# A gated spatial mixing stage as one unrolled pipeline over eight PSUM banks, with post norms begun in the tails of the stages

## What is computed

```python
h = h + rmsnorm(y, post_g)              # post norm 0, after the mLSTM mixer
hn = rmsnorm(h, pre_g)                  # "pre1"
p = einsum('bsd,de->bse', hn, w_in)     # 1024 -> 3 x 2048
u, v, z = split(p)
u = gelu(u)
v = rmsnorm(gelu(v), sg_norm_g)         # over all 2048 columns
vg = v.reshape(B, 4, 128, 8, 256)       # 4 chunks of tokens, 8 groups of columns
wm = w_spatial * causal                 # 8 x 128 x 128
vs = einsum('gts,bcsgd->bctgd', wm, vg) + b_spatial
y = u * vs * silu(z)
y = einsum('bse,ed->bsd', y, w_out)     # 2048 -> 1024
h = h + rmsnorm(y, post_g)              # post norm 1, then out
```

## Time and profile before

| | us |
|---|---|
| median of 3 runs | 3165.85 (3164.73 to 3171.25) |
| the profiled execution | 3168.81 |
| its span | 3166.9 |
| TensorE busy in the span | 2781.3 (88%) |
| VectorE, ScalarE, GpSimd busy | 1460.2, 1097.8, 756.3 |

### The profile page before, as it was taken

How to read it: one execution, slowest core, us unless ns; L and a number is a source line. 1 busy time by engine, 2 the same in 40 slices (tenths; PEclk the granted TensorE clock), 3 DMA queues, 4 the chain that set the end, 5 groups by cost and what they waited for, 6 DMA issues and landing times. The chain is left out here.

```text
span 3166.9 us, 40378 instructions
## 1 busy us (share of the span) xinstructions
PE 2781.3 (88%) x15916; PEld 2249.8 (71%) x15916; DVE 1460.2 (46%) x2541; ACT 1097.8 (35%) x1836; POOL 756.3 (24%) x168
## 2 busy tenths in 40 slices
PE   5889999769999995999879999689988995889995
PEld 3777877658888884766557878477767883877774
DVE  4335354443343345556544344455565456234444
ACT  3444445332222222455432222344433342432222
POOL 1101111012222221111024443222222331233331
PEclk9999999979999996999989999899999997899997
DMA  5123223101111111122112221222211220122221
GB/s 216 54 104 105 108 104 116 61 34 67 66 53 66 66 40 61 57 92 81 54 53 93 94 92 66 83 67 67 67 61 54 80 80 28 66 94 79 79 69 51
DMA packets 54293, 239.72 MB, mean 76 GB/s; under 512 B 4116, under 2 KB 22036, under 8 KB 29848
## 3 DMA queue, kind: packets, MB, share of 16 engines
q1 hardware_dynamic: 54168, 237.99, 21.8%
HBM read 235.87 MB, written 2.10 MB: 75 GB/s over the span
## 5 line engine op out<-in xcount | busy, mean ns | idle before, releaser
L262 PE MATMUL bank<-u_hi,w_hi 128*128 128x512 f32 (+1 forms) x1856 | 711.2, 383 | 66.4 <-DVE u_lo L396 41.7
L230 POOL TENSOR_TENSOR w_lo<-w_raw,w_hi 128x2048 fp32r<-128x2048 f32 x97 | 446.9, 4607 | 1115.8 <-ACT w_hi L225 1115.8
L263 PE MATMUL bank<-u_lo,w_hi 128*128 128x512 f32 (+1 forms) x1856 | 693.2, 374 | 0.0
L264 PE MATMUL bank<-u_hi,w_lo 128*128 128x512 f32 (+1 forms) x1856 | 691.8, 373 | 0.0
L262 PEld LDWEIGHTS bank<-u_hi,w_hi 128*128 128x128 f32 x1856 | 358.3, 193 | 161.6 <-issue 59.7
L264 PEld LDWEIGHTS bank<-u_hi,w_lo 128*128 128x128 f32 x1856 | 358.5, 193 | 61.1
L263 PEld LDWEIGHTS bank<-u_lo,w_hi 128*128 128x128 f32 x1856 | 359.5, 194 | 57.5 <-issue 2.2
L225 ACT ACTIVATE w_hi<-w_raw 128x2048 fp32r<-128x2048 f32 x97 | 185.5, 1912 | 397.4 <-PE bank L264 395.5
L701 DVE SCALAR_TENSOR_TENSOR resid<-bank,mod,resid 128x512 f32<-128x512 f32 (+1 forms) x384 | 242.4, 659 | 171.3 <-PE bank L264 169.4
L262 PE MATMUL bank<-hid_hi,w_hi 128*128 128x512 f32 (+1 forms) x768 | 276.4, 360 | 3.7 <-DVE resid L701 3.7
L263 PE MATMUL bank<-hid_lo,w_hi 128*128 128x512 f32 (+1 forms) x768 | 273.7, 356 | 0.0
(11 more groups left out here) (364 smaller groups left out, 4583.2 us busy)
## 6 DMA issues: line engine op xcount, KB each, us to landing
w_raw<-stream SPq DMA_DIRECT2D x185, 1024.0 KB, 4.8
w_raw<-stream SPq DMA_DIRECT2D x44, 512.0 KB, 4.4
bias<-bias SPq DMA_DIRECT2D x8, 896.0 KB, 6.8
ada_more<-stream SPq DMA_DIRECT2D x4, 1024.0 KB, 11.3
resid<-h SPq DMA_DIRECT2D x1, 3072.0 KB, 10.3
out<-resid SPq DMA_DIRECT2D x1, 2048.0 KB, 7.3
w_raw<-stream SPq DMA_DIRECT2D x4, 256.0 KB, 3.6
cos_sin<-cst SPq DMA_DIRECT2D x1, 512.0 KB, 7.9
```

The costliest lines, as they stand in the source:

```text
L230: pool.tensor_tensor(m.wl[:, s, 0:width], m.raw[:, s, 0:width], m.wh[:, s, 0:width].bitcast(F32), ALU.subtract).then_inc(m.lo_split, 1)
L262: pe.matmul(out, lh, rh, start=start, stop=False)
L263: pe.matmul(out, lh, rl, start=False, stop=False)
L264: return pe.matmul(out, ll, rh, start=False, stop=stop)
```

## The change

1. **Post norms.** The separate `post_stage` blocks go. In the tail of `mlstm_stage` and in that of the odd stage ScalarE squares each tile of y as soon as VectorE has added it; GpSimd adds the squares of tiles 0 to 5; three ones matmuls sum acc and the squares of tiles 6 and 7; Ln and Exp follow. The products `y * gain * rstd` and `h + y` of post norm 0 stand at the start of the odd block, one tile ahead of one another.
2. **One block for the odd stage**, all unrolled, with `Linear` over eight banks. ScalarE splits chunk 1 first, then squares each tile of h as VectorE finishes it; eight ones matmuls accumulate these squares in one bank. The values of group 0 run with k as the outer loop and wait for `u_lo` tile by tile. Gelu of v writes to `v` directly.
3. **Groups.** TensorE's order is u(i), x(i), z(i), wo(i-1). VectorE stages group i+1 between its products for group i. ScalarE waits for wo(i-1) before it makes y's high half of group i, which now lies, with the low half, in the unused token columns of `m.uh` and `m.ul`.
4. **Output.** SP stores each tile of h (256 KB) as soon as it is final, eight DMAs in place of one.
5. Semaphore counts run on from `mlstm_stage` into the odd stage (`shared`, `spent`). ScalarE waits for both look-ahead chunks (64) before the look-ahead split.

```diff
+class Stats:
+    def square(self, act, k, tile):
+        if k >= 3:
+            act.wait_ge(*self.added(k - 2))
+        act.activation(self.sq[k % 2] if k else self.acc, tile, ACT.Square).then_inc(self.m.st_squared.sem)
+    def add(self, pool):
+        for k in range(1, 6):
+            pool.wait_ge(*self.squared(k))
+            if k > 1:
+                pool.wait_ge(*self.added(k - 1))
+            pool.tensor_tensor(self.acc, self.acc, self.sq[k % 2], ALU.add).then_inc(self.m.st_added.sem)
+    def sum(self, pe, outs):
+        pe.wait_ge(*self.added(5))
+        for x, part in enumerate((self.acc, self.sq[0], self.sq[1])):
+            if x:
+                pe.wait_ge(*self.squared(5 + x))
+            for out, cut in outs:
+                ins = pe.matmul(out, cst(self.m, "ones"), cut(part), start=(x == 0), stop=(x == 2))
+        ins.then_inc(self.m.st_summed.sem)
...
 def mlstm_stage(nc, m):
                 act.wait_ge(*used(len(fills) - 2))
-                split_hi(act, m, 0, 2, None)
+                act.wait_ge(*m.ahead_in.at(64))
+                act.activation(m.wh[:, 0, :], m.raw[:, 0, :], ACT.Copy).then_inc(m.ahead_hi.sem)
+                for k in range(KT):
+                    act.wait_ge(*lin.read(use["wo", H - 1, k]))
+                    post.square(act, k, quarters(m.y[:, k, :]))
+                post.root(act, quarters(lin.out(use["post",])))
...
+def odd_stage(nc, m, post0, out):
+        fills = [("v", g) for g in range(G)]
+        for i in range(G):
+            fills += [("u", i), ("z", i)] + ([("wo", i - 1)] if i else [])
+        fills += [("wo", G - 1)]
...
+                for k in range(KT):
+                    sp.wait_ge(*post_h.at(KT + k + 1))
+                    sp.dma_start(out[:, k, :], m.h[:, k, 0:LAT]).then_inc(m.out_done, 16)
...
+                act.preload_act_table_set(EXP_SET)
+                act.wait_ge(*m.ahead_in.at(64))
+                high(1)
+                for k in range(KT):
+                    act.wait_ge(*post_h.at(k + 1))
+                    act.activation(sq[k], m.h[:, k, 0:LAT], ACT.Square).then_inc(squared.sem)
...
+                    high(fill["z", i] + 2)
+                    if i:
+                        act.wait_ge(*used(fill["wo", i - 1]))
+                        high(fill["wo", i - 1] + 2)
+                    act.wait_ge(*y_done.at(2 * i + 2))
+                    act.activation(yh, y4, ACT.Copy).then_inc(y_high.sem)
...
+                for i in range(G):
+                    spatial(i)
+                    if i + 1 < G:
+                        stage(i + 1)
+                    gate(i)
+                    if i:
+                        for k in range(KT):
+                            add(i - 1, k)
+                    low(i)
...
+                for k in range(KT):
+                    pe.wait_ge(*squared.at(k + 1))
+                    ins = pe.matmul(lin.out(use["sum",]), cst(m, "ones"), sq[k], start=(k == 0), stop=(k == KT - 1))
+                ins.then_inc(lin_done.sem)
+                for g in range(G):
+                    values(g)
+                for i in range(G):
+                    project_group("u", i)
+                    mix(i)
+                    project_group("z", i)
+                    if i:
+                        project_out(i - 1)
+                project_out(G - 1)
```

More of the change, by code:

```diff
@@ L2693, in mlstm_stage @@
             order += [("q", i + 1), ("k", i + 1), ("v", i + 1, 0), ("v", i + 1, 1)] if i + 1 < H else []
-        order += [("wo", H - 1, n) for n in range(KT)]
+        order += [("wo", H - 1, n) for n in range(KT)] + [("post",)]
         use = {y: n for n, y in enumerate(order)}
@@ L3231, in _ @@
                 project_out(H - 1)
+                n = use["post",]
+                pe.wait_ge(*lin.before(n))
+                post.sum(pe, [(lin.out(n), lambda t: t)])
+        for s in range(2):
+            m.spent(f"chunk_in{s}", 16 * len(range(2 + s, len(fills), 2)))
+        for name in ("chunk_hi", "chunk_lo"):
+            m.spent(name, len(fills) - 1)
+        m.spent("lin_done", len(order) - 1)
+        for b in range(8):
+            m.spent(f"lin_free{b}", len(range(b, len(order) - 1, 8)))
@@ L3241, in post_stage @@
         rstd = sb("rstd", [P, LAT])
[L3242 to L3300, removed]
+        staged = sb("staged", [P, NC, GD])
@@ new lines, in odd_stage, with used, lower @@
+        for i in range(G):
+            order += [(x, i, j) for x in "uxz" for j in range(2)]
+            order += [("wo", i - 1, k) for k in range(KT)] if i else []
+        order += [("wo", G - 1, k) for k in range(KT)] + [("last",)]
+        use = {x: n for n, x in enumerate(order)}
+        def used(n):
+            kind, i = fills[n]
+            last = {"v": 1 if i else NC - 1, "u": 1, "z": 1, "wo": KT - 1}[kind]
+            return lin.ready(use[kind, i, last])
+        def lower(n):
+            return chunk_lo.at(n)
@@ new lines, in project_group @@
+                def project_group(kind, i):
+                    pe.wait_ge(*lower(fill[kind, i]))
+                    wh, wl = columns(m.wh, kind, i), columns(m.wl, kind, i)
+                    for j in range(2):
+                        n, c = use[kind, i, j], slice(j * P, j * P + P)
+                        pe.wait_ge(*lin.before(n))
+                        for k in range(KT):
+                            ins = mm3(pe, lin.out(n), wh[:, k, c], wl[:, k, c], m.uh[:, k, 0:LAT], m.ul[:, k, 0:LAT],
+                                      k == 0, k == KT - 1)
+                        ins.then_inc(lin_done.sem)
@@ new lines, in mix @@
+                def mix(i):
+                    pe.wait_ge(*staged_done.at(i + 2))
+                    for j in range(2):
+                        n = use["x", i, j]
+                        pe.wait_ge(*lin.before(n))
+                        for c in range(NC):
+                            ins = pe.matmul(lin.out(n)[:, c * P:c * P + P], staged[:, c, j * P:j * P + P], wm[:, i, :],
+                                            start=True, stop=True)
+                        ins.then_inc(lin_done.sem)
@@ L3495, in program @@
+                project_out(G - 1)
+                n = use["last",]
+                pe.wait_ge(*lin.before(n))
+                post1.sum(pe, [(lin.out(n), lambda t: t)])
+    finish_stage(m, 32, 0)
 def program(nc, ins, out):
```

462 lines of the change are left out of this document (269 added, 193 removed).

## The result

The changed kernel takes a median of 3068.37 us (3066.78 to 3073.53, 4 runs) against 3165.29 (3163.64 to 3171.25, 4 runs) for the kernel before. The ratio is 0.9693 (95% interval 0.9676 to 0.9711), or 96.9 us less. The prediction said 3072 and 93 less. Runs of the same kernel differ by up to 8 us here. The profiled execution took 3066.78, its span 3065.0, and TensorE was busy 2765.5 us, 90% of it.

What follows compares the result with a forecast made beforehand. TensorE was taken as the engine to watch, held up by waits and slower matmuls after them. Gains 25.5 + 54.9 + 13.0 = 93.4 give span 3073.5, program 3075.4, less 3.0 for the median: 3072 us, range 3063 to 3089.

Steps and rivals of the forecast that it cites:

- Part 1: mLSTM's tail and post norm 0: rstd 4.2 us after the last update, h complete at 2675.6 (profile time).
- Rival (a): Norm tails: GpSimd's adds cost far more than a quarter split; 3105 us at 4.6 each, 3082 at 2.3; chance 0.08.
- The block boundary: Between mLSTM's tail and the odd block: VectorE's first instruction 1.2 us after the old block ends.
- The collision: Post norm 0: GpSimd's split of chunk 1 falls among VectorE's products and stalls them, 4.2 us charged, 0 as other end.
- Part 2: Odd stage's norm and first values, fed tile by tile by u_lo, ending 2694.5; gain 25.5 us up to here.
- Part 3: Loop over groups: 34.4 us per group, TensorE waiting only before the last output projection; 279.6 us, gain 54.9.
- The single wait: Before wo(7), the last output projection: TensorE waits for y's halves, 2.5 us plus 0.5 for the clock.
- The chunk ring: Groups: each weight chunk's split, 6.5 us once its slot is free, is ready in time; 3.8 us slack at the tightest.
- (b): Groups: the chunk ring doesn't fit, one split per group 3 us late, 24 us in all, 3096 us; chance 0.07.
- (c): Groups: the overlap fails, wo still waits for y_lo in each group, some 45 us, 3117 us; chance 0.05.
- rival (d): Unbroken 357 us stretch: TensorE's clock drops, slower than before from 94 us at the lower level; chance 0.02.
- Part 4: Final tail: 4.2 us to rstd, 11.2 products and sums, 3.8 last store; 19.2 against 32.2, gain 13.0.

Runs made afterwards that it cites:

- e5: Changed kernel with each GpSimd add of squares in the two tails preceded by an unused second one; update to end 431.9 us against 416.0, program 3089.67.
- e1: Changed kernel with ScalarE's split of chunk 1 moved behind its eight u_hi copies; update to end 413.2 us against 416.0, program 3070.57.
- e4: Changed kernel with the values of group 0 waiting for the last u_lo before their first matmul; update to end 423.8 us against 416.0, program 3086.91.
- e2: Changed kernel with each output projection back in its own group, after its z; groups 327.6 us against 278.3, program 3118.06.
- e7: Changed kernel with two buffers for y's halves and y_lo amid the updates; groups 275.5 us against 278.3, program 3070.91.
- e3: As e2, plus 14 matmuls with overwritten results in each wait for y_lo; groups 314.2 us against e2's 327.6, program 3107.65.
- e6: Changed kernel with the output stored by one 2 MB DMA at the end; tail 22.4 us against 17.4, program 3077.17.
- after: The changed kernel itself, without any follow-up alteration; update to end 416.0 us, median 3068.37 us.

## Why the prediction held, point by point

**Part 1.** The term for rstd was 4.2 after the last update. The last step, an Exp, ended at 2653.70, so 4.66. GpSimd's add, for which no row stood, took 1.29 at a pitch of 1.41. The five adds in a row above show it (7.04 us), and so does the line's own summary, changed kernel (durations, ns min/median/max):

```profile
L2665 POOL TENSOR_TENSOR resid<-resid x10: 1286/1292/1305, 2642.3 to 3046.6; 128x512 f32<-128x512 f32 x10
```

That is the upper end of the 1.15 to 1.3 that I took from the split by the count of columns. The pitch is a little over the 1.36 of a tile, so the adds don't quite keep up and TensorE waits 0.50 for the last; I had put nothing there, and that is the 0.5 by which rstd came late. By the estimate of 1.1 from the Trainium skill, "GPSIMD Engine Reference", "Elementwise — side-by-side cycle accounting", that wait would not be there; the measured 1.29 decides. Rival (a) had the mechanism right and nothing of it happened, because the add is short. Its price left something out: it had "about 5 and 5" for adds of 2.3 each. In e5, with about 2.6 each, the wait grew by 6.1 in each tail, which is of that size, but the ones matmuls at the lower level added 2.2 each time.

The block boundary took 0.31 (2653.70 to 2654.01), not 1.2. Products and sums took 14.4 (2654.01 to 2668.46), where I had 11.2 + 4.2 = 15.4. The collision cost 4.25 (4.99 against 0.74), as the earlier trace rows had it. A tile's product and sum, now a tile apart from one another, took 1.27 where the 11.2 has 1.4; over eight tiles that is 1.0. The Trainium skill, "SBUF — State Buffer", "SBUF: two separate sides", says that GpSimd and VectorE hold their shared ports as an exclusive lock for an instruction. The product that ends at 2663.5, half a microsecond after the split, agrees with it. e1 took the split away and got 4.26 back.

**Part 2.** h was expected 20.8 after the update and came at 19.4. From h to the first value matmul the prediction had 5.7 (2675.6 to 2681.3), and it took 5.7 (2668.46 to 2674.17). The sums of squares ran at the lower level in part, yet TensorE waited 7.0 before and among them for ScalarE, so they hid under the stream that feeds them, as charged. The wait for the last u_lo, 14.4 before, is the 3.6 for the first one, and the overlap of values and u_lo is worth 7.8 to 9.2 (e4). The values of group 0 took 14.5 instead of the 13.2 charged. Gelu begins at 2687.58, when the first of four tiles is ready, and the last follows 1.1 later; the matmuls ran at the lower level until 2680.1, 5.9 us on. In e2 and e7 they did so for 2.7 and 3.0 us, and gelu came 1.4 earlier. So the 1.4 won at h was given back here, and the gain is 25.5, as predicted, by two small errors that cancel. That is luck: by the other runs with the same code in this part (e2, e3, e6, e7) the gain is 26.4 to 27.0. Of the 25.5, e4 shows 8 to 9 for the overlap of values and u_lo. No run puts the sums of squares back onto VectorE, so the share of the norms' new order rests on the marks of the two traces alone.

**Part 3.** A group was to take 34.4 and takes 34.44. The single wait was to be 2.5 and is 2.45. The 0.5 put down for slower matmuls after it was nothing in this execution and 1.6 in e1 and e6. The sum in this part gives 279.3, and the 279.6 that it goes on with has no reason beside it. The chunk ring holds, and rivals (b) and (c) did not happen: there is no TensorE wait for w_lo or for y_lo within a group. The prediction split the gain in 28.3 for waits, 5.5 for the gap before u, and 21.1 for slower matmuls and turns of the banks. The first two are as the rows have them. The third I can now split in part: it measured 22.0 (55.9 less 28.4 and 5.5). Most of it is the clock. After one of the waits, kernel before, in order of time on TensorE:

```profile
2875.61 0.79 PE L262 MATMUL bank<-y_hi,w_hi 128*128 128x512 f32 x1 [3.85 <-DVE y_lo L3457]
2876.20 0.63 PE L263 MATMUL bank<-y_lo,w_hi 128*128 128x512 f32 x1
2876.63 0.63 PE L264 MATMUL bank<-y_hi,w_lo 128*128 128x512 f32 x1
...
2880.83 0.39 PE L262 MATMUL bank<-y_hi,w_hi 128*128 128x512 f32 x1
2881.06 0.39 PE L263 MATMUL bank<-y_lo,w_hi 128*128 128x512 f32 x1
```

At the lower level the matmuls start every 0.43 us instead of every 0.23, so 47% of that time is lost. Between the gelu of the last values and the last update the kernel before spent 44.3 us at the lower level, in nine stretches, with TensorE busy for 37.3 of them. That is 17 us lost. The same working for e2 (34.1 us at the lower level, busy for 29.1) gives 13.6, and filling the waits gave 13.4 back. So 17 of the 22.0 are the clock. Of the remaining 5, e2 still has 2 with its eight banks (15.6 less 13.4). The other 3 fit the turns of four double banks, but no run changed the banks alone, so that is argued only. The price of rival (c) doesn't follow from its words: seven waits of 3.9 "and as much again" would be 55, not 45. In e2 the eight waits, of 4.53 each there, cost 49.3. Against rival (d) speaks the granted clock, which stayed at 1.00 for 375 us, from 2680.4 to 3055.7.

**Part 4.** This is where I was off most, 14.7 instead of 13.0. rstd cost 4.7 for 4.2, products and sums 10.2 for 11.2, and the last store 2.5 for 3.8. The store was priced by a load of 256 KB at 3.6, and a store of the same size lands in 2.0.

**The sum.** 96.1 against 93.4, or 3 us of 3068. The mis-sized terms are the store (1.3), the boundary (0.9) and the products (1.0 in each of two norms), and against them rstd (0.5 twice) and the first values (1.3). The groups were 1.0 better than their term. The median came 3.6 under the forecast, and that holds two errors that cancel in part. The profiled execution came 8.6 under its forecast of 3075.4, with 5.75 of it ahead of the change. And it lay 1.6 under the median, where I had put the median 3.0 under it.

## What to carry to other kernels

When a projection waits for a chain on other engines, put the previous round's projection behind the next round's independent work: here it was worth 49 of 56 us, of which 34 were the wait and 16 the slower matmuls after it, and filling the wait with matmuls that nobody needs got only 13 back. Before a GpSimd instruction is moved, look which products of VectorE it will lie beside: a 4.6 us split cost 4.3 us on the path here, and moving it behind them, by one line, was worth 2.9 net. Compare stretches inside the traces from a common mark, since the same instructions came up to 12 us earlier or later ahead of it.

## What the hardware did that I had not expected

- After one wait of 2.45 us the granted clock stayed at 1.00 in three runs (after, e4, e5) and fell to the lower level in two (e1, e6), with the same code in this place; it is worth 1.6 us. In e2, with 4.53 us, each wait cost about 2 us more than itself. After 6.6 us (e5) six passes of the ones matmul took 5.02 for 2.81.
- Fourteen matmuls of 512 columns whose results nobody uses, in each wait of e3, kept the granted clock at 1.00, where e2 shows 0.95.
- When VectorE's products and GpSimd's split met, both lost: the product 4.25 us, the split 1.06 (5.66 for 4.6).
- A store of 256 KB lands in 2.0 us, a load of the same size in 3.2 to 3.6 (medians of each run).
